# A fused transformer kernel on one core: rows of x loaded ahead of the first conditioning block, dense steps placed between the halves of conditioning groups

## What is computed

```python
sh_l, sc_l, gt_l = modulation(c, w_ada, b_ada)          # silu(c) @ w_ada + b_ada, split in 3
sh_c, sc_c, gt_c = modulation(c_ctx, w_ada, b_ada)
h_l = rmsnorm(x_lat, g_pre) * (1.0 + sc_l[:, None, :]) + sh_l[:, None, :]
h_c = rmsnorm(x_ctx, g_pre) * (1.0 + sc_c) + sh_c
...
k_c, v_c = ...                                           # h @ w_in[:, 1024:1536]: keys and values
```

## Time and profile before

| what | us |
|---|---|
| median of 3 runs | 1559.55 (1559.46 to 1567.86) |
| the profiled execution | 1564.55 |
| its span, first to last instruction | 1562.7 |

### The profile page before, as it was taken

One profiled execution on the slowest core, in us unless ns is written; L12 is line 12 of the kernel. 1 busy time (PEld: TensorE's weight loads), 2 busy tenths in 40 slices (PEclk: granted clock), 3 DMA queues, 4 the chain that ended last, 5 costly groups with the idle time before them and its releaser, 6 DMA issues.

```text
span 1562.7 us, 24142 instructions
## 1 busy us (share of the span) xinstructions
PE 1469.1 (94%) x9392; PEld 1204.4 (77%) x9392; DVE 993.5 (64%) x2286; ACT 754.6 (48%) x1630; POOL 67.5 (4%) x76
## 2 busy tenths in 40 slices
PE   6999999999999999999979999897999899999999
PEld 4777766777778777888757777576787798799987
DVE  4647677565566648535684677666777476777763
ACT  4436566453655443331143555555566347455542
POOL 0000000100000100020010100001101020000000
PEclk9999999999999999999989999899999999999999
DMA  9121180222560332221461253333435542445554
GB/s 362 55 108 55 57 316 21 102 82 67 189 230 1 108 102 81 94 68 54 170 221 54 76 159 102 139 98 126 162 125 155 197 161 95 149 148 189 189 189 135
DMA packets 59866, 202.84 MB, mean 130 GB/s; under 512 B 7694, under 2 KB 10984, under 8 KB 59624
## 3 DMA queue, kind: packets, MB, share of 16 engines
q1 hardware_dynamic: 53568, 192.84, 35.5%
q10 hardware_dynamic: 6008, 7.40, 2.1%
q0 software_dynamic: 176, 1.06, 0.2%
HBM read 199.43 MB, written 1.84 MB: 129 GB/s over the span
## 4 chain that ended last, share of the span: by engine, by line
PE 72%; DVE 15%; ACT 5%; DMA 4%; issue 3%; POOL 1%; SPq 0%; ACTq 0%; POOLq 0%; DVEq 0%
PE ps L2243 66%; PE ps L2246 5%; DVE w_l L2913 3%; DVE st L3012 1%; ACT w_h L2556 1%; DVE l_P L2917 1%; DVE x L2921 1%; DMA w_l_ada<-in_l_ada 1%; DMA w_raw<-in_l_out 1%; DVE m_P L3496 1%; ACT l_P L2559 1%; DVE l_xn L2917 1%; DVE l_h_lat L2921 1%; DMA w_raw<-in_l_ada 1%; POOL mstat L3590 1%
## 5 line engine op out<-in xcount | busy, mean ns | idle before, releaser
L2913 DVE TENSOR_TENSOR w_l<-w_raw,w_h 128x1024 fp32r<-128x1024 f32 (+3 forms) x263 | 315.4, 1206 | 74.9 <-ACT w_h L2556 74.4
L2556 ACT ACTIVATE w_h<-w_raw 128x1024 fp32r<-128x1024 f32 (+3 forms) x263 | 272.1, 1042 | 109.6 <-DMA w_raw<-in_f_down 25.3
L2243 PE MATMUL ps<-w_h,l_hTh 128*128 128x512 f32 (+1 forms) x384 | 156.2, 407 | 0.5 <-DVE w_l L2913 0.4
L2243 PE MATMUL ps<-w_h,l_hTl 128*128 128x512 f32 (+1 forms) x384 | 151.8, 395 | 0.0
L2243 PE MATMUL ps<-w_l,l_hTh 128*128 128x512 f32 (+1 forms) x384 | 151.8, 395 | 0.0
L2559 ACT ACTIVATE l_P<-ps,st 128x512 f32<-128x512 f32 (+1 forms) x128 | 77.6, 608 | 91.5 <-DVE st L2921 64.2
L3012 DVE TENSOR_REDUCE st<-ps 128x1 f32<-128x512 f32 (+2 forms) x112 | 72.7, 649 | 43.9 <-PE ps L2243 43.7
L2243 PE MATMUL ps<-f_hTh,w_h 128*128 128x256 f32 x352 | 99.2, 282 | 0.0
L2243 PE MATMUL ps<-f_hTl,w_h 128*128 128x256 f32 x352 | 99.1, 281 | 0.0
L2243 PE MATMUL ps<-f_hTh,w_l 128*128 128x256 f32 x352 | 99.0, 281 | 0.0
L2243 PE MATMUL ps<-l_hTh,w_h 128*128 128x512 f32 (+1 forms) x264 | 97.5, 369 | 0.5 <-issue 0.5
(11 more groups left out here) (444 smaller groups left out, 3467.9 us busy)
## 6 DMA issues: line engine op xcount, KB each, us to landing
w_raw<-in_l_ada SPq DMA_DIRECT2D x49, 512.0 KB, 5.3
w_raw<-in_l_z SPq DMA_DIRECT2D x32, 512.0 KB, 3.5
w_raw<-in_l_adg SPq DMA_DIRECT2D x32, 512.0 KB, 3.9
w_raw<-in_l_out SPq DMA_DIRECT2D x32, 512.0 KB, 4.7
w_raw<-in_m_merge SPq DMA_DIRECT2D x24, 512.0 KB, 3.3
w_raw<-in_f_gate SPq DMA_DIRECT2D x22, 512.0 KB, 3.3
w_raw<-in_f_up SPq DMA_DIRECT2D x22, 512.0 KB, 3.2
w_raw<-in_f_down SPq DMA_DIRECT2D x22, 512.0 KB, 4.2
```

The source lines that it names most:

```text
L2243: return p.e.matmul(out, lhsT, rhs, start=start, stop=stop)
L2556: return p.e.activation(out, a, func, scale=scale)
L2913: return p.e.tensor_tensor(out, a, b, op)
```

## The change

Two places are edited. In `layer_first` the loop over kp is rewritten: in every round the pending conditioning result and the rows' transposes come first, then the split of one more weight block, then two blocks of the next conditioning group, the dense step for this same kp, and the other two blocks. Before, a round took all four blocks of its group, the split, the transposes, and then the dense step of the kp before. In `begin_loads` the load of x tile 0 is queued ahead of conditioning block 0 and x tile 1 ahead of block 1, and the ctx tiles come behind those two blocks. The 16th conditioning block becomes the fourth of the ring instead of the third.

```diff
@@ layer_first
         for kp in range(4):
-            if kp:
-                drain(upto(mod, 4))
-                p.W.split_more()
             late.pop()()
             r.at(LAT, kp)
             r.at(CTX, kp)
-            if kp:
-                drain(upto(kv, 4))
-        p.W.split_more()
+            p.W.split_more()
+            drain(upto(mod, 2))
+            drain(upto(kv, 4))
+            drain(upto(mod, 2))
         drain(kv)
@@ begin_loads
+        def rows(t):
+            src = n.dram["x"] if t < 2 else n.dram["ctx"]
+            src = src.rearrange("a t d -> (a t) d")[(t % 2) * 128:(t % 2) * 128 + 128, :]
+            p.e.dma_start(n.X[:, t, :], src).then_inc(*p.landed("d_x", t))
+
         for x, b in enumerate(blocks):
+            if x < 2:
+                rows(x)
             if x in (4, 8, 12):
                 p.w_load(x // 4 - 1)
             p.e.dma_start(b.tile[:], n.w[b.name][b.i]).then_inc(*p.landed("d_aside", b.i))
-            if x < 4:
-                src = n.dram["x"] if x < 2 else n.dram["ctx"]
-                src = src.rearrange("a t d -> (a t) d")[(x % 2) * 128:(x % 2) * 128 + 128, :]
-                p.e.dma_start(n.X[:, x, :], src).then_inc(*p.landed("d_x", x))
+            if x < 2:
+                rows(2 + x)
```

## The result

The changed kernel takes 1570.36 us (median of 10 runs) against 1559.51 us (median of 10 runs of the kernel before). The medians lie 10.9 us apart; the ratio estimated from all the runs is 1.0063, with a 95% interval from 1.0046 to 1.0079, which is 9.8 us more, 7.2 to 12.3. The forecast was 1568.0 us, 8.3 to 8.5 us more. The profiled execution has a span of 1568.7 us.

A forecast was written before the change was run, and what follows sets the result against it. PE's queue was taken to bound the kernel; +6.3 us for the last dense step's later start and +2.0 for the clock make +8.3, 1568 us on the median of 1559.55. Range for 8 in 10: 1562 to 1575 us.

The forecast's parts named there:

- What bounds it: Whole kernel: PE, busy 94% of the span, bounds it; a delay in the first dense phase is carried to the end.
- Rival (c): After 58 us: some stall absorbs the delay, giving 1560 us; chance 0.08.
- rival (b): Loop over kp: the affine chain is covered, 1559 to 1560 us, at most 0.6 us won; chance 0.07.
- (a): Start: clock already up at the first dense step, or A3 not late; +6.3 or +7.0, 1566 to 1567 us; chance 0.20.
- Step 1: Loads at the start: A3 goes from seventh to eighth place, and the first hT is ready 1.27 us later.
- Step 2: Start of the first dense step: it comes forward by 0.97 us, to 24.80 from 25.77.
- Step 3: Loop over kp: PE waits 1.26, 1.26 and 2.24 us for hT ahead of the last three dense steps; +6.3 us.
- Step 4: First dense step: it opens at the slow clock level, +2.0 us, between bounds of nothing and 5.0 us.
- Rival (d): New waits: PE falls back to the slow level, half of each later dense step slow, 7.5 us more, 1575; chance 0.10.
- The sum: Whole kernel: +6.3 for the last dense step's later start and +2.0 for the clock make +8.3 us.

The follow-up runs named there:

- e1: The changed order of the loads alone, with the loop of the kernel before; ratio to the kernel before 1.0002 (0.9983 to 1.0021).
- e2: The new loop over kp alone, with the loads in the order of the kernel before; ratio to the kernel before 1.0044 (1.0026 to 1.0063).
- e10: Kernel before, with one tile of the previous dense step ahead of the transposes in the last two rounds, split behind the rows' calls; ratio 1.0017 (1.0000 to 1.0033).
- e4: The changed kernel, but the dense step between two half groups is that of the kp before; ratio 1.0029 (1.0007 to 1.0050).
- e9: The changed kernel with all four next conditioning blocks between transposes and dense step, and two weight blocks split at kp = 1; ratio 1.0015 (1.0001 to 1.0030).
- e11: The changed kernel with the rows' two calls exchanged, ctx tiles ahead of x tiles; V copied at 66.85 us, 7.1 us later than in the changed kernel.
- e12: The kernel before with the rows' two calls exchanged, ctx tiles ahead of x tiles; V copied at 50.53 us.
- e7: The changed kernel run once more, nothing altered; V copied at 60.36 us.
- e6: The changed kernel with two more matmuls, result unused, on PE between the last transposes and the last dense step; V copied at 60.52 us.
- e3: The changed kernel with all four blocks of the next conditioning group between transposes and dense step; V copied at 58.19 us, ratio 1.0051 (1.0030 to 1.0072).

## Why the prediction was right, step by step

**What bounds it.** Right. The 8.56 us lost by V are still 8.56 at 98.89 us and 9.26 at 304.82. Rival (c), absorption, is out. So is rival (b), which needed less than 1.94 us from turn to hT, and (a) with its clock already up at D0: D0 opens slow in every trace with this loop and halves.

**Step 1, the loads.** The mechanism holds (the fourth tile's square waits behind the stage row, and that for A3). A3's matmuls moved by 0.76 us instead of 1.27. Over all traces A3's matmuls begin at 15.2 to 15.4 with the old order, and once at 16.25, and at 16.1 to 16.7 with the new one. A single landing scatters by nearly as much as the step is worth: the distances within a trace fit the queue's order (A2 to A3 2.55 us with a ctx tile between them, 1.28 without), only the whole stream came 0.5 us earlier in the trace of after. e1 shows that in the old loop it is worth nothing. In the new one the hT of D0 hangs on it, 0.74 us between e2 and the changed kernel.

On the Trainium skill's sentence that completion isn't FIFO per issuing engine ("DMA: Bandwidth & Descriptors", "Queues, rings and completion order"): no landing looked at here overtook one issued before it. A2's and A3's matmuls begin 2.55 to 2.58 us apart in the six traces with the old order of loads and 1.27 to 1.29 us apart in the eight with the new one, which is plain order. The beat isn't even, though: A7 had landed at 23.0 in both the trace of before and that of e10, but the next load, kv's second block, at 24.2 in one and at 25.8 in the other.

**Step 2.** D0 begins 1.36 us ahead of before instead of 0.97, which is mostly step 1's error again. PE waits 1.40 us for the hT and not 2.1, since A4 and A5 take 1.93 us at the slow pace and not about 1.

**Step 3, the latency behind each turn, +6.3.** This is the step that carries the sum, and the runs bear it out: waits of 1.10, 1.10 and 2.11 us against 1.26, 1.26 and 2.24; a period of 10.55 against 10.34. Turn to dense step takes 3.31 us (33.02 to 36.33) against 3.2. The period is 0.2 us longer, half of it because a half group takes 1.08 us and not 0.98, half because of the latency; the waits are shorter since transposes and blocks take 2.2 us and not 1.94. e4 takes the waits away and wins 6.7 us back, 2.0 of them the clock's; e9 shortens three of them (that ahead of D0 too) and wins some 4.6 us beside what the clock gave, with the stage row's wait in it; e11 lengthens them by 1.07 us and e12 shows that the same exchange is free where the lag covers it. That last pair is the strongest: same edit, no instruction more, 7 us in one order (4.3 without the clock) and none in the other.

What the sum left out is what e4 shows, some 0.35 us for each group that is cut in two. Of that only the 0.10 us of the half group behind D k stand in the changed kernel's period; the rest falls into the stretch that the latency sets anyway.

**Step 4, the clock in D0, +2.0.** That D0 would open slow was right; the 2.0 was a choice between bounds and not worked out, and that it fits is luck. D0 to D1 takes 11.92 us, 1.37 over the later period. In e7, e6 and e2, with the same loop, it takes 12.45, 13.06 and 13.31, so 1.4 to 2.8 in all: the 2.0 lies in the middle, and the upper bound of 5.0 was far. A slow matmul of 512 columns was reckoned at 0.44 us and takes 0.43.

On the Trainium skill's "TensorE: Matmul & The Clock Gate", "What's actually happening", that the throttled state is the default: the trace agrees, since PE's work is at the slow pace from the first conditioning blocks on (1.08 us for 16 matmuls), and D0's first six matmuls still are.

**Rival (d), given 0.10, was true in one of its three places.** I argued against it from an idle of 1.74 us that was followed by fast matmuls. That was one draw: PE idles 1.72 to 1.74 us at this same place in eleven of the traces, and in seven of them the dense matmuls behind are slow. The timeline of e12's PE:

```profile
56.29 1.30 PE L2246 MATMUL ps<-identr,l_qs 128*128 128x128 f32 x8 [1.73 <-DVE l_qs L2913]
57.40 0.76 PE L2243 MATMUL ps<-w_h,l_hTh 128*128 128x512 f32 x1
57.95 0.63 PE L2243 MATMUL ps<-w_l,l_hTh 128*128 128x512 f32 x1
58.38 0.63 PE L2243 MATMUL ps<-w_h,l_hTl 128*128 128x512 f32 x1
```

The waits of 1.1 us ahead of D1 and D2 indeed cost nothing. But ahead of D3 PE idled 2.11 us, and the clock fell within D3's first tile in both traces of the changed kernel. It cost 0.65 us up to V (59.77 - 57.44 is 2.33; in e2, where it didn't fall, it is 1.68) and some 1.5 us of PE time in all, not the 2.5 that (d) put on each. What came after V was covered, as the distance at 98.89 us shows.

**The sum.** To D3's start it was 8.3 us in the prediction and 57.44 - 49.61 = 7.8 in the trace; with the slower D3 it is 8.56 at V. That this lies so near 8.3 is in part luck: D0 came 0.4 us earlier and its clock cost 0.6 less than reckoned, three periods took 0.6 more, and the fall at D3, which the sum had at nothing, added 0.7. The timed runs give 9.8 (7.2 to 12.3), which holds both; 1570.36 lies within the forecast's own 1565 to 1571. Some 0.7 us more appear between 203 and 221 us, where both chains go through landings of conditioning weights; why they are later there was not tried.

## What to carry to other kernels

Before a step is moved next to its producer, add up the chain between them over all engines and ask what PE has to do in the meantime: here 3.3 us of transpose, add, affine and split against 2.2 us of cover ahead of D1 and D2, and against 1.2 ahead of D3. Filling a wait for DMA at the start by pulling a dense step forward can win at most that wait, once; giving up a lag of one step pays its latency in each round. And when calls that "only ask for more" (a split, a prefetch) change their place, read each engine's queue again: a rounding that waits for its landing ahead of a small copy made PE wait 2.99 us in e10 where it had waited 0.40, and a split spent on the wrong block made it wait 2.38 us in e3.

## What the runs showed of the hardware

The granted clock fell after idle times of PE of about two microseconds and less. In the loop over kp, idle times of 2.1 to 3.2 us in one piece were followed by a fall to 1.2 GHz in eight places (D3 in both traces of the changed kernel, D2 and D3 in e3, D1 to D3 in e11, turn 1 in e10) and not in two (D3 in e2 and in e9). After the eight waits of 1.10 or 1.11 us ahead of D1 and D2 in e2, e6, e7 and the changed kernel it never fell. In between, the idle time of 1.72 to 1.74 us ahead of the queries' second transposes was followed by a fall in seven traces (e1 to e6 and e12) and not in four (both of before, e9 and e10). So the length of the one idle time doesn't decide; what does was not tried. A fall in D1, D2 or D3 costs about 1.5 us of PE time (eight matmuls at 0.43 us instead of 0.23).

The column of the granted clock reads 1.00 for the first 24 us, while PE's rows there show the slow pace (16 matmuls in 1.08 us instead of 0.62). For the start of an execution the durations have to be read, not the column.

The landings at the very start scatter: the kernel before got its seventh load, A3, 0.9 us later in one trace than in another, and kv's second block landed at 24.2 us in its first trace and at 25.7 in e12, which has the same loads. Milestones should be compared from a common event (D0, a turn), not from zero.
